# Modulation tiles regrouped: none in steps 16 to 27 of the input projection, ten groups of four ahead of steps 28 to 37, with the weight split of those steps moved

## The chip, the cores and the metric

One core of one Trainium2 chip. The metric is the device time in microseconds (us) of one execution of the kernel; lower is better.

## The reference, cut to what matters

One layer of a diffusion backbone, on 128 context and 256 latent tokens (T = 384 columns, three blocks of 128 rows) of width 2048:

```python
mod = silu(cond) @ w_mod + b_mod                 # 2048 -> 6*2048, for two conditioning vectors
sh_m, sc_m, g_m, sh_f, sc_f, g_f = split(mod, 6)
h = rmsnorm(x, g0) * (1 + sc_m) + sh_m
u = h @ w_in                                     # 2048 -> 5120
m = concat(diff_attention, rg_lru, neighbourhood_attention, gqa)(u)
x = x + g_m * rmsnorm(m @ w_out, g1)
h = rmsnorm(x, g2) * (1 + sc_f) + sh_f
a, g = split(h @ w_ffn_in, 2)
x = x + g_f * rmsnorm((silu(g) * a) @ w_ffn_out, g3)
```

All is f32. The large matmuls split each operand into a high part that the fast f32 format holds exactly and the remainder, and add three products: high times high, low times high, high times low.

## The kernel before, in words

**Weight tiles.** All weights come as 284 tiles of 1 MB (128 partitions, 4 x 512 values each), in the order of a list, PLAN (lines 94 to 110). SyncE issues one DMA for each (line 441), in that order, into a ring of six buffers, raw. Ahead of each it waits until the tile that had the buffer is used up (lines 427 to 433). So a transfer that must wait holds back all behind it. The buffer of a tile is the one freed longest ago (tile_slots, line 122), which in this stretch is that of six tiles earlier.

**The steps.** Input and output projection are 56 steps of one GEMM tile each (STEPS). Steps 0 to 15 do the first four column blocks with k outermost; from 16 on a column block takes four steps. Steps 40 to 55 are the output projection. A step from 4 on (step_tile, line 914) is 36 matmuls of 512 columns: for each of three row blocks tb, four k and three products (lines 934 to 936). Behind each row block comes a "gap" with whatever attention work stands in a hand-made table, GAPS (line 149): gap g = 3s + tb. Before its first matmul the step waits for both halves of the split tile.

**The split.** hi (line 452) is ScalarE's: two copies of 128x1024 from raw to whi, a ring of two tiles. lo (line 1218) is VectorE's: two subtractions raw - whi, written over the raw buffer as wlo. In the loops over s (lines 666 and 1541) both engines run, in this order: the third gap of step s-1; the eviction of modulation rows (ScalarE, rows_out, if a group ends in this step) or the convolution of the recurrence (VectorE); hi or lo of tile s+1; the other work of the step; gap(s, 0), and on VectorE mod_out; gap(s, 1). Each engine takes its instructions in this order.

**Modulation.** mod is made in 22 groups; group m from 4 on has four tiles of 1 MB, each used by four matmuls of 32 weight columns x 512 (mod_tile, line 798; each is two instructions in the profile), side by side in four parts of the array. mod_tiles (line 84) says which tiles stand ahead of step s: four in steps 2 and 3, two in each of steps 4 to 35. When a group is complete, ScalarE copies it (rows_out, line 463), TensorE turns it with four transposes (mod_turn, line 811) behind the first row block of that step, and VectorE reduces it to modc (mod_out, line 1273). From group 10 on all groups use PSUM bank 3, and the first tile waits until the group before is in modc (line 802). Groups 12 to 21 are not needed before step 39.

**Recurrence and attention.** Steps 16 to 27 also carry the RG-LRU recurrence: four rounds of three steps. TensorE turns its input ahead of the first step of round 0 and behind steps 18, 21 and 24 (lru_turn, line 979: six transposes; the first waits until VectorE has added the partial sums of step 15, part_add, line 1359). The gates' matmuls (lru_gates, line 991) come behind steps 16, 19, 22 and 25. VectorE runs lru_conv (1373), lru_decay (1385) and lru_scan (1404) in the three steps of a round, each behind or ahead of the lo of its step; ScalarE its tanh, exp and sqrt; GpSimd gelu, norms and rope. Attention starts at gap 85 (step 28). Once head group D is done (gap 108, in step 36) GpSimd issues the load of kvC and sixteen small loads of the bias table.

Of the kernel before, what the change touches and what calls it, by code (L numbers as in the profile page):

```python
# [32 lines left out]
KG = 4  # L33
# [16 lines left out]
KH = KD // 2  # L50
KG2 = FK // KG
EARLY = 4
IN_STEPS = IN_N * KG
OUT_N = D // NC
OUT_KG = [1, 3, 0, 2]
STEPS = IN_STEPS + OUT_N * KG

FINE = 4
MOD_K0 = [16, 0, 18, 2] + [4 * j for j in [5, 1, 6, 2, 7, 3] + list(range(8, 20))]
# [10 lines left out]
def in_step(s):  # L70

    return (s % EARLY, s // EARLY) if s < EARLY * KG else (s // KG, s % KG)


def step_key(s):

    if s < IN_STEPS:
        return ("in",) + in_step(s)
    if s < STEPS:
        return ("out", s % OUT_N, OUT_KG[(s - IN_STEPS) // OUT_N])  # L80
    return ("up", 0, 0)


def mod_tiles(s):

    if s < 2:
        return 0, []
    if s < EARLY:
        return FINE + s - 2, [0, 1, 2, 3]
    m, first = 4 + s // 2, s % 2 * 2  # L90
    return (m, [first, first + 1]) if m < len(MOD_K0) else (0, [])


def tile_plan():
# [54 lines left out]
def attention_gaps():  # L149
# [23 lines left out]
    for h in range(4):  # L173
        conv[TB * IN_STEPS + h] = ("D", h)
        conv[TB * IN_STEPS + 18 + h] = ("A", h)
    return {g: [task[1:] for task in sorted(tasks)] for g, tasks in gaps.items()}, conv
# [9 lines left out]
CONV_NO = {_key: _i for _i, (_g, _key) in enumerate(sorted(CONV.items()))}  # L186
A_SCALE = {TB * IN_STEPS + 14 + _h: _h for _h in range(4)}
K_SLOT = [0, 0, 1, 1] + [hd % 2 for hd in range(4, 12)]
# [9 lines left out]
def build(nc, wst, xt_d, x_p, x_s, cdiff, cna, cgqa, c, c_ctx, lam_w, gate_w, na_rpb, qk_g, par_d, tables_d,  # L198
# [101 lines left out]
    with ExitStack() as ctx:  # L300
# [94 lines left out]
        def in_bank(s, tb):  # L395

            return (4 if s < EARLY * KG and s % 2 else 0) + tb

# [4 lines left out]
        def last_step(n):  # L403

            return EARLY * (KG - 1) + n if n < EARLY else KG * n + KG - 1

        GATES_AT = {("in",) + in_step(EARLY * KG + 3 * i): i for i in range(4)}

        ENDS = {}
        for st in range(STEPS):  # L410
            if st < EARLY * KG or st >= IN_STEPS or st % KG == KG - 1:
                ENDS[st] = len(ENDS)
# [38 lines left out]
        def _(act):  # L451
# [26 lines left out]
            def part_out(n):  # L478

                for tb in range(TB):  # L480
                    if tb < TB - 1:
                        act.wait_ge(acc_ps, 2 * n + tb + 1)
                    else:
                        act.wait_ge(w_used, used(*step_key(n // 2 * 2 + 1)) - 1 + n % 2)
                    nc.scalar.activation(U[:, n, tb, :], ps[4 * (n % 2) + tb][:, :], ACT.Copy).then_inc(part_a, 1)
# [180 lines left out]
            for s in range(STEPS):  # L666
                i, phase = (s - EARLY * KG) // 3, (s - EARLY * KG) % 3
                lru = 0 <= i < 4
                m, kgs = mod_tiles(s)
                if s > EARLY * KG:  # L670
                    gap(s - 1, 2)
                if s == 0:
                    rows_out(2)
                    rows_out(3)
                    hi(*step_key(1), bs=(0,))
                    h_shift(2)
                    h_shift(3)
                    hi(*step_key(1), bs=(1,))
                if s == 1:
                    part_out(0)  # L680
                    part_out(1)
                if KG - 1 in kgs:
                    rows_out(m)
                if s == 3:
                    for k in range(KG, 2 * KG):
                        h_shift(k)
                if lru and phase == 0:
                    lru_in(i)
                if s:
                    hi(*step_key(s + 1))  # L690
                if s == EARLY * KG:
                    act.wait_ge(l_setup, 2)
                if s == 3:
                    part_out(2)
                    part_out(3)
                if s in (7, 11):
                    for k in range(s + 1, s + 1 + KG):
                        h_shift(k)
                if lru and phase == 1:
                    lru_gates(i)  # L700
                if lru and phase == 2:
                    lru_sqrt(i)
                if s == EARLY * KG:
                    act.wait_ge(lam_p, 1)
                    nc.scalar.activation(lamt[:, 2:4], lamt[:, 0:2], ACT.Exp).then_inc(lam_e, 1)
                    act.wait_ge(part_d, TB * EARLY * (KG - 1))
                    norm_squares(2, DK, 12, 0)
                if s == EARLY * KG + 2:
                    norm_squares(4, DQ, 0, 6)
                if s in (IN_STEPS - 2, IN_STEPS - 1):  # L710
                    act.wait_ge(w_used, used("in", IN_N - 1, 1))
                    for n in range(2 * (s % 2), 2 * (s % 2) + 2):
                        nc.scalar.activation(h_hi[:, 4 + n, :].rearrange("p (t f) -> p t f", f=P),
                                             u3(BX + n * P, P), ACT.Copy).then_inc(mb_hi, 1)
                if s >= EARLY * KG:
                    gap(s, 0)
                    gap(s, 1)
# [489 lines left out]
        def _(dve):  # L1207
# [10 lines left out]
            def lo(*key, bs=(0, 1)):  # L1218

                t = TILE[key]  # L1220
                g = GEMM_NO[t]
                for b in bs:
                    dve.wait_ge(w_hi, 2 * g + b + 1)
                    V.tensor_tensor(wlo[:, 2 * SLOT[t] + b], raw_of(t)[:, HK * b:HK * b + HK].rearrange("p k n -> p (k n)"),  # L1224
                                    whi[:, 2 * (g % RING) + b].bitcast(F32), ALU.subtract).then_inc(w_lo, 1)
# [315 lines left out]
            for s in range(STEPS):  # L1541
                i, phase = (s - EARLY * KG) // 3, (s - EARLY * KG) % 3
                lru = 0 <= i < 4
                m, kgs = mod_tiles(s)
                n = s - (STEPS - OUT_N)
                if s > EARLY * KG:
                    gap(s - 1, 2)
                if n >= 0:
                    diagonal(G_M, n, 0, 2 * n + 1)
                if s in (2, 3):  # L1550
                    mod_out(m)
                    if s == 2:
                        dve.wait_ge(xr_ok, 1)
                        col_scaled(KG, KG, m).then_inc(xs_ok, 1)
                    else:
                        for k in range(KG, 2 * KG):
                            first_h(k)
                if lru and phase == 0:
                    lru_conv(i)
                if s:  # L1560
                    lo(*step_key(s + 1))
                if n > 0:
                    for tb in range(TB):
                        y1_gate(n - 1, tb)
                if KG - 1 in kgs and EARLY <= s < EARLY * KG:
                    mod_out(m)
                    if m < 10 and m % 2 == 0:
                        dve.wait_ge(xr_ok, m // 2 - 1)
                        col_scaled(KG * (m // 2 - 1), KG, m).then_inc(xs_ok, 1)
                if s == 2:  # L1570
                    softplus()
                if s in (7, 11):
                    for k in range(s + 1, s + 1 + KG):
                        first_h(k)
                if EARLY <= s < EARLY * KG:
                    part_add(s)
                if s >= EARLY * KG:
                    gap(s, 0)
                    if KG - 1 in kgs:
                        mod_out(m)  # L1580
                if lru and phase == 1:
                    lru_decay(i)
                if lru and phase == 2:
                    lru_scan(i)
                if s in (IN_STEPS - 2, IN_STEPS - 1):
                    for b in range(2 * (s % 2), 2 * (s % 2) + 2):
                        dve.wait_ge(mb_hi, b + 1)
                        V.tensor_tensor(h_lo[:, 4 + b, :].rearrange("p (t f) -> p t f", f=P), u3(BX + b * P, P),
                                        h_hi[:, 4 + b, :].rearrange("p (t f) -> p t f", f=P).bitcast(F32),
                                        ALU.subtract).then_inc(mb_lo, 1)  # L1590
                if s == IN_STEPS + 7:
                    dve.wait_ge(mod_col, len(MOD_K0))
                    gain(G_M, 1, False)
                    gain(SC_F, 2, True)
                if s >= EARLY * KG:
                    gap(s, 1)
                if -1 <= n < OUT_N - 1:
                    diagonal(G_M, n + 1, 1, 2 * n + 2)
# [379 lines left out]
```

## Time and profile before

| what | value |
|---|---|
| median of 3 runs | 1799.8 us (1799.41 to 1800.14) |
| the profiled execution, its own time | 1798.27 us |
| its span, first to last instruction | 1796.4 us |
| TensorE (PE) busy, share of the span | 1763.2 us, 98% |
| VectorE (DVE) busy | 947.0 us, 53% |
| ScalarE (ACT) busy | 659.8 us, 37% |
| mean granted TensorE clock | 0.999 |

PE rows are matmuls, PEld rows weight loads, POOL is GpSimd. Matmuls are pipelined: a row's duration is longer than the distance to the next one, so a run of matmuls is read by start to start. In rows of the timeline the brackets at the end give the engine's idle time before the row and what ended it.

### The profile page before, as it was taken

The page shows a single profiled execution, that of the slowest core. Times are in us where ns is not written, and L with a number is a line of the kernel's source. Part 1 is how long each engine was busy: PE and PEld are TensorE (multiplying, and loading weights), DVE is VectorE, ACT ScalarE, POOL GpSimd, SP SyncE. Part 2 cuts the span into 40 slices and gives each one's busy share as a digit, 9 for nine tenths or more (in the row PEclk, how much of TensorE's full clock was granted, in tenths as well). Part 3 has the DMA queues.
Part 4 walks back from the last instruction along what each step waited for, and adds up shares of the span by engine and source line. Part 5 has one row for each costly group of instructions (what it writes and reads, how often), then busy time and mean ns, then how long its engine had stood idle before and what let it go on. Part 6 is the DMA issues. An engine that isn't in the chain of part 4 may idle for free.

```text
span 1796.4 us, 22651 instructions
## 1 busy us (share of the span) xinstructions
PE 1763.2 (98%) x9499; PEld 1526.4 (85%) x9499; DVE 947.0 (53%) x1276; ACT 659.8 (37%) x952; POOL 125.9 (7%) x172
## 2 busy tenths in 40 slices
PE   5999999999999999999999999999999999999998
PEld 4667666677778879999999999999999988888886
DVE  5554578633657677356656633333333455555554
ACT  3422354443464344222222222222222344454542
POOL 1001045420300010000000000000000000000000
PEclk9999999999999999999999999999999999999999
DMA  9988777775322242345454443433333333333331
GB/s 395 349 331 318 299 270 273 294 265 228 114 104 94 104 177 117 118 172 203 167 207 188 182 147 117 140 118 124 135 117 140 119 124 134 117 138 121 121 113 71
DMA packets 47046, 317.37 MB, mean 177 GB/s; under 512 B 5433, under 2 KB 7665, under 8 KB 10017
## 3 DMA queue, kind: packets, MB, share of 16 engines
q1 hardware_dynamic: 44592, 305.35, 45.4%
q0 software_dynamic: 2288, 10.56, 1.8%
q8 instruction: 75, 1.23, 0.3%
q14 instruction: 27, 0.21, 0.0%
q10 hardware_dynamic: 64, 0.02, 0.0%
HBM read 310.52 MB, written 5.39 MB: 176 GB/s over the span
## 4 chain that ended last, share of the span: by engine, by line
PE 93%; DVE 3%; DMA 2%; ACT 1%; issue 0%; POOL 0%; SPq 0%; DVEq 0%; POOLq 0%; ACTq 0%
PE ps L1158 41%; PE ps L934 7%; PE ps L936 7%; PE ps L935 7%; PE ps L828 7%; PE ps L829 7%; PE ps L827 7%; PE ps L806 3%; DMA raw<-in_weights 2%; PE ps L1048 1%; PE ps L1071 1%; DVE wlo L1224 1%; PE ps L1106 1%; PE ps L894 1%; PE ps L896 1%; PE ps L895 1%
## 5 line engine op out<-in xcount | busy, mean ns | idle before, releaser
L1224 DVE TENSOR_TENSOR wlo<-raw,whi 128x1024 fp32r<-128x1024 f32 x376 | 459.8, 1236 | 692.6 <-ACT whi L460 692.1
L460 ACT ACTIVATE whi<-raw 128x1024 fp32r<-128x1024 f32 x376 | 392.3, 1058 | 829.7 <-PE ps L1158 507.0
L1158 PE MATMUL ps<-h_hi,whi 128*128 128x384 f32 x1408 | 471.4, 335 | 0.5 <-DVE h_lo L1303 0.5
L1158 PE MATMUL ps<-h_hi,wlo 128*128 128x384 f32 x1408 | 470.4, 334 | 0.0
L1158 PE MATMUL ps<-h_lo,whi 128*128 128x384 f32 x1408 | 470.3, 334 | 0.0
L1158 PEld LDWEIGHTS ps<-h_hi,whi 128*128 128x128 f32 x1408 | 264.3, 188 | 0.7 <-issue 0.7
L1158 PEld LDWEIGHTS ps<-h_lo,whi 128*128 128x128 f32 x1408 | 264.3, 188 | 0.0
L1158 PEld LDWEIGHTS ps<-h_hi,wlo 128*128 128x128 f32 x1408 | 264.3, 188 | 0.0
L934 PE MATMUL ps<-whi,h_hi 128*128 128x512 f32 x624 | 259.8, 416 | 0.2 <-DVE wlo L1224 0.2
L936 PE MATMUL ps<-wlo,h_hi 128*128 128x512 f32 x624 | 244.5, 392 | 0.0
L935 PE MATMUL ps<-whi,h_lo 128*128 128x512 f32 x624 | 243.6, 390 | 0.0
L827 PE MATMUL ps<-whi,j_hi 128*128 128x512 f32 x516 | 204.0, 395 | 0.0
L829 PE MATMUL ps<-wlo,j_hi 128*128 128x512 f32 x516 | 200.9, 389 | 0.0
L828 PE MATMUL ps<-whi,j_lo 128*128 128x512 f32 x516 | 200.9, 389 | 0.0
L934 PEld LDWEIGHTS ps<-whi,h_hi 128*128 128x128 f32 x624 | 117.2, 188 | 54.6 <-issue 28.7
L936 PEld LDWEIGHTS ps<-wlo,h_hi 128*128 128x128 f32 x624 | 117.1, 188 | 25.9
L935 PEld LDWEIGHTS ps<-whi,h_lo 128*128 128x128 f32 x624 | 117.5, 188 | 25.1 <-issue 1.9
L828 PEld LDWEIGHTS ps<-whi,j_lo 128*128 128x128 f32 x516 | 96.9, 188 | 21.9 <-issue 1.9
L827 PEld LDWEIGHTS ps<-whi,j_hi 128*128 128x128 f32 x516 | 96.9, 188 | 21.8 <-issue 1.9
L829 PEld LDWEIGHTS ps<-wlo,j_hi 128*128 128x128 f32 x516 | 96.9, 188 | 20.1
L1635 DVE TENSOR_TENSOR j_lo<-h3T,j_hi 128x1536 fp32r<-128x1536 f32 x44 | 77.4, 1758 | 8.4 <-ACT j_hi L762 8.4
L1855 POOL TENSOR_TENSOR smalls<-smalls 128x3 f32<-128x3 f32 x2 | 0.4, 188 | 1027.0 <-ACT ps L725 998.2
(257 smaller groups left out, 1363.6 us busy)
## 6 DMA issues: line engine op xcount, KB each, us to landing
raw<-in_weights SPq DMA_DIRECT2D x278, 1024.0 KB, 4.9
raw_x<-in_weights SPq DMA_DIRECT2D x6, 1024.0 KB, 18.5
xT<-in_x_t SPq DMA_DIRECT2D x4, 768.0 KB, 7.0
out<-x_sb SPq DMA_DIRECT2D x6, 512.0 KB, 2.7
x_sb<-in_x_sample POOLq DMA_DIRECT2D x1, 2048.0 KB, 11.0
sbc<-silu_rows POOLq DMA_DIRECT2D x1, 2048.0 KB, 8.2
gw<-in_lru_gate_w SPq DMA_DIRECT2D x4, 256.0 KB, 3.3
out<-U POOLq DMA_DIRECT2D x4, 256.0 KB, 5.6
```

What stands on the lines that cost most here:

```text
L460: nc.scalar.activation(whi[:, 2 * (g % RING) + b], raw_of(t)[:, HK * b:HK * b + HK].rearrange("p k n -> p (k n)"), ACT.Copy).then_inc(w_hi, 1)
L806: ins = nc.tensor.matmul(ps[mod_bank(m)][32 * kk:32 * kk + 32, :], stat[:, 2 * k:2 * k + 32], raw_of(t)[:, kk, :], start=(kg == 0), stop=( ...
L827: nc.tensor.matmul(acc, xh[:, kk + HK * b, xs], wh[:, cols], start=(k == 0), stop=False)
L828: nc.tensor.matmul(acc, xl[:, kk + HK * b, xs], wh[:, cols], start=False, stop=False)
L829: ins = nc.tensor.matmul(acc, xh[:, kk + HK * b, xs], wl[:, cols], start=False, stop=(k == k_last))
L894: nc.tensor.matmul(acc, h_hi[:, k, xs], wh[:, cols], start=(k == 0), stop=False)
L934: nc.tensor.matmul(acc, h_hi[:, k, xs], wh[:, cols], start=begin, stop=False)
L935: nc.tensor.matmul(acc, h_lo[:, k, xs], wh[:, cols], start=False, stop=False)
L936: ins = nc.tensor.matmul(acc, h_hi[:, k, xs], wl[:, cols], start=False, stop=end)
L1158: return nc.tensor.matmul(ps[bank][:, 0:T], w[:, k % KH * P:(k % KH + 1) * P], xs[:, k, :], start=first, stop=last)
L1224: V.tensor_tensor(wlo[:, 2 * SLOT[t] + b], raw_of(t)[:, HK * b:HK * b + HK].rearrange("p k n -> p (k n)"), whi[:, 2 * (g % RING) + b].bitc ...
L1635: V.tensor_tensor(j_lo[v % 2][:, :, :], h3T[:, KG * q:KG * q + KG, :], j_hi[v % 2][:, :, :].bitcast(F32), ALU.subtract).then_inc(jl, 1)
```

## The change

It changes mod_tiles: steps 4 to 15 keep two tiles each, steps 16 to 27 have none, and steps 28 to 37 have all four tiles of groups 12 to 21. PLAN, the order of the transfers and the buffers follow from it; the number of tiles, matmuls and transposes is the same. And for tiles 29 to 37 hi and lo are no longer issued one step ahead, but in the tile's own step, right behind the third gap of the step before: on ScalarE ahead of rows_out. Tile 38 is split one step ahead again, in step 37, behind tile 37.

```diff
@@ -50,6 +50,8 @@
 EARLY = 4
+FOURS = EARLY * KG + 12
+FOURS_END = FOURS + 9
 IN_STEPS = IN_N * KG
@@ -87,8 +89,9 @@
         return 0, []
     if s < EARLY:
         return FINE + s - 2, [0, 1, 2, 3]
-    m, first = 4 + s // 2, s % 2 * 2
-    return (m, [first, first + 1]) if m < len(MOD_K0) else (0, [])
+    if FOURS <= s <= FOURS_END:
+        return 12 + s - FOURS, [0, 1, 2, 3]
+    return (4 + s // 2, [s % 2 * 2, s % 2 * 2 + 1]) if s < EARLY * KG else (0, [])
@@ -679,6 +682,8 @@  (ScalarE)
                 if s == 1:
                     part_out(0)
                     part_out(1)
+                if FOURS <= s - 1 < FOURS_END:
+                    hi(*step_key(s))
                 if KG - 1 in kgs:
                     rows_out(m)
@@ -686,7 +691,7 @@
                 if lru and phase == 0:
                     lru_in(i)
-                if s:
+                if s and not FOURS <= s < FOURS_END:
                     hi(*step_key(s + 1))
@@ -1557,7 +1562,9 @@  (VectorE)
                 if lru and phase == 0:
                     lru_conv(i)
-                if s:
+                if FOURS <= s - 1 < FOURS_END:
+                    lo(*step_key(s))
+                if s and not FOURS <= s < FOURS_END:
                     lo(*step_key(s + 1))
```

## Rows read from the trace of the kernel before

**Rows 1.** The page: span and busy time.

```profile
span 1796.4 us, 22651 instructions
PE 1763.2 (98%) x9499; PEld 1526.4 (85%) x9499; DVE 947.0 (53%) x1276; ACT 659.8 (37%) x952; POOL 125.9 (7%) x172
```

**Rows 2.** Waits of PE, 200 to 470 us: us in total, times, longest.

```profile
PE ps L1061 <- DVE pb L1460: 1.8, 1, 1.8
PE ps L806 <- DVE modc L1280: 1.2, 1, 1.2
```

**Rows 3.** Timeline of PE in step 15: start, duration, engine, line.

```profile
192.50 1.93 PE L806 MATMUL ps<-raw,stat 128*32 128x512 f32 x16
194.35 0.50 PE L934 MATMUL ps<-whi,h_hi 128*128 128x512 f32 x1
...
195.84 0.60 PE L815 MATMUL ps<-par,modrow 128*128 128x128 f32 x4
196.20 0.48 PE L934 MATMUL ps<-whi,h_hi 128*128 128x512 f32 x1
```

**Rows 4.** Timeline of PE in step 3, four modulation tiles in a row.

```profile
64.17 1.92 PE L806 MATMUL ps<-raw_x,stat 128*32 128x512 f32 x16
65.91 1.90 PE L806 MATMUL ps<-raw,stat 128*32 128x512 f32 x16
67.74 0.50 PE L894 MATMUL ps<-whi,h_hi 128*128 128x512 f32 x1
```

**Rows 5.** Timeline of PE, steps 16 and 17, start of steps 28 and 29.

```profile
203.22 1.92 PE L806 MATMUL ps<-raw,stat 128*32 128x512 f32 x16
205.08 0.87 PE L988 MATMUL ps<-par,U 128*128 128x128 f32 x6
205.71 0.47 PE L934 MATMUL ps<-whi,h_hi 128*128 128x512 f32 x1
...
214.00 2.77 PE L998 MATMUL ps<-lru_xc,gw 128*128 128x388 f32 x8
216.70 1.93 PE L806 MATMUL ps<-raw,stat 128*32 128x512 f32 x16
...
343.34 1.93 PE L806 MATMUL ps<-raw,stat 128*32 128x512 f32 x16
...
354.40 1.93 PE L806 MATMUL ps<-raw,stat 128*32 128x512 f32 x16
```

**Rows 6.** Timeline of DVE: step 15's sums, lo of tiles 21, 22, 23.

```profile
202.49 1.88 DVE L1371 TENSOR_TENSOR U<-U,ps 128x512 f32<-128x512 f32 x3
...
255.05 2.36 DVE L1224 TENSOR_TENSOR wlo<-raw,whi 128x1024 fp32r<-128x1024 f32 x2 [6.62 <-ACT whi L460]
...
270.77 3.44 DVE L1224 TENSOR_TENSOR wlo<-raw,whi 128x1024 fp32r<-128x1024 f32 x2
...
282.88 2.35 DVE L1224 TENSOR_TENSOR wlo<-raw,whi 128x1024 fp32r<-128x1024 f32 x2
```

**Rows 7.** Timeline of ACT and then DVE in step 30: hi and lo.

```profile
371.48 2.01 ACT L460 ACTIVATE whi<-raw 128x1024 fp32r<-128x1024 f32 x2 [4.94 <-DMA raw<-in_weights]
...
372.58 2.36 DVE L1224 TENSOR_TENSOR wlo<-raw,whi 128x1024 fp32r<-128x1024 f32 x2 [7.32 <-ACT whi L460]
```

**Rows 8.** Timeline of PE: the tiles ahead of steps 30 and 33.

```profile
366.16 1.92 PE L806 MATMUL ps<-raw,stat 128*32 128x512 f32 x16
...
406.83 1.92 PE L806 MATMUL ps<-raw,stat 128*32 128x512 f32 x16
```

**Rows 9.** Timeline of ACT: last work of gaps 89, 98, 107.

```profile
366.27 0.28 ACT L592 ACTIVATE pT<-ps 128x128 f32<-128x128 f32 x1 [1.21 <-PE ps L1061]
...
408.20 0.19 ACT L603 ACTIVATION_READ_ACCUMULATOR pb<-ps,smalls 128x1 f32 x1
...
448.10 2.00 ACT L460 ACTIVATE whi<-raw 128x1024 fp32r<-128x1024 f32 x2
```

**Rows 10.** Windows: us, PE, PEld, DVE, ACT, POOL busy, PEclk, DMA share, GB/s.

```profile
10.00:20.00 10.00, 5.23 (x88) 4.01 (x92) 6.87 (x7) 3.47 (x5) 0.00 (x0) 1.00 1.02 427
```

**Rows 11.** DMA queue of GpSimd, 445 to 465 us: packets, MB, share.

```profile
q0 software_dynamic: 656, 1.57, 34.0%
```

## The prediction

> **What bounds the kernel now.** I read the page first: TensorE is busy for 98% of the span [rows 1]. Then the waits of PE: from step 16 to step 37 it waits for other engines for little more than 3 us, the two entries shown and one of 0.4 us [rows 2]. So the kernel is bound by TensorE, and what the change can gain is TensorE time itself; what it can lose is any wait that it opens, in full, since nothing later has slack to take it back. Then the timelines of PE, ACT and DVE, step by step, to see what each step costs TensorE and how far ahead of it the split runs.
>
> **The change part by part.** All terms are against the profiled execution (its own time 1798.3 us, span 1796.4 us). That is 1.5 us under the median of the runs.
>
> *TensorE work taken out of steps 16 to 27.* From 203.22 to 343.34 us it takes 140.1 us [rows 5]. A bare step is 205.71 to 214.00, 8.3 us; twelve make 99.5. The four input turns at 0.63 (205.08 to 205.71) make 2.5, the four gate groups at 2.70 (214.00 to 216.70) make 10.8 [rows 5]. What is left, 27.3 us, is what the modulation takes there: 24 tiles, six turns of a group, and the 1.2 us wait of a first tile for modc [rows 2]. It all goes: **-27.3**.
>
> *The same work in steps 28 to 37.* Two tiles take 1.85 us start to start [rows 3], four in a row 3.57 (64.17 to 67.74) [rows 4]. Eight steps go from two to four, 8 x 1.72 = 13.8; steps 36 and 37 get four, 7.1; six more groups turn there, each 0.36 and a slower first matmul, about 0.44 [rows 3], 2.6. **+23.5**. The net of both is -3.8: fewer runs of these tiles, each with its way in and out, and the lost wait. That is the whole gain.
>
> *The first input turn loses its cover.* Now two tiles run from 203.22 to 205.08 while VectorE adds the sums of step 15, which end at 202.49 + 1.88 = 204.37 [rows 5, 6]. Without them the turn could start at 203.2 and has to wait for 204.4: **+1.2**. Between nothing and 1.9 (the cover's whole length).
>
> *VectorE in the recurrence.* Its work of one round, here the second, runs almost without a break from lo of tile 21 at 255.05 to the end of lo of tile 23 at 285.23: 30.2 us [rows 6], of which about 1.5 is idle or mod_out. Call it 28.7. TensorE's round loses its tiles and shrinks to 3 x 8.3 + 0.6 + 2.7 = 28.2 us. So VectorE, with slack now, becomes about even, and late in the rounds in which GpSimd works beside it. lo of tile 22 comes behind the whole of lru_decay, then scan and convolution stand ahead of lo of tile 23 and of the gates' matmuls. Following both engines' orders by these durations I get 1.3 us lost at step 22, about 1 us at the gates behind it, less than 1 us in the third round, nothing in the first and last. The splits themselves don't wait for transfers there (one tile a step). I take **+2.0**; from 0 (slack at the start of each round suffices) to 6 (2 in each of three rounds).
>
> The row of tile 22 shows two subtractions in 3.44 us where 2.36 is usual [rows 6], beside GpSimd's norm. The Trainium skill, SBUF — State Buffer, section "SBUF: two separate sides", says that a VectorE operation with two SBUF inputs and a GpSimd operation lock each other out for a whole instruction; the trace agrees in kind, at 1.1 us for the pair. If every GpSimd operation of a round cost VectorE its full length, it would be the second rival below.
>
> *The split moved behind the gap.* This is the large term. TensorE leaves the third gap of step s-1 and starts on the four tiles at once; call that T. It is ready for the step at T + 3.57 [rows 4]. From the start of hi to the end of lo it takes 371.48 to 374.94, 3.46 us [rows 7]. So hi would have to start at T + 0.1, but ScalarE has the gap's work first. In step 30 the last copy ends 0.4 us after T (366.27 + 0.28 against 366.16) [rows 8, 9]: 0.2 lost. In step 33 the exponential of the gap ends at 408.39, 1.56 after T = 406.83 [rows 8, 9]: 1.4 lost. Behind gap 107, with two exponentials, hi can start at 448.10 [rows 9], 1.7 after the gap: 1.6 lost. Read in this way for the nine steps 29 to 37, the losses are 0.4, 0.2, 1.0, 1.4, 1.4, 0.4, 0.2, 1.6, 0.7: **+7.5**. From 5 (some of these waits overlap with others) to 9 (lo stretched by GpSimd in two or three steps, 1.1 each).
>
> *Transfers.* Steps 28 to 37 now need five tiles each instead of three. At full load the queues move 427 GB/s [rows 10], 2.5 us for a tile. A tile alone takes 5.3 us from the freed buffer (about 366.1) to hi at 371.48 [rows 7, 8]. In the new order the first tile for the next step is freed when the step before ends, and the fifth, the one to split, lands four tiles later: 5.3 + 10 = 15.3 us after it. A step of this stretch takes 13.4 to 13.8 us now (from 366.16 to 406.83 three steps, 13.6 each) [rows 8], and 15.3 to 16 with two more tiles and its wait; hi is wanted about 1 us later still. That just holds. It does not hold for tile 29: step 28 takes 11.06 [rows 5], then 13.2, so the tile lands 1.5 us late, and the load of kvA falls there too: **+2.0**, from 0 to 4. And it does not for tile 37: when head group D is done in step 36, GpSimd's loads take 34% of the engines' time over 20 us, 6.8 us [rows 11], and some 3 of them fall ahead of tile 37, with 1 of slack: **+2.0**, from 0 to 6.
>
> The Trainium skill, DMA: Bandwidth & Descriptors, section "Anatomy of one DMA", gives about 2.0 us plus bytes over 436 GB/s for one DMA, 4.4 us for a tile. By that estimate the fifth tile would land at 14.0, tile 29 would be in time, and the sum about 1.5 smaller; the 5.3 read here includes SyncE's wait and issue, so I keep it.
>
> *At nothing.* The wait of 1.8 us in step 37 [rows 2] comes from GpSimd's bias addition beside VectorE; that falls into the same step again. rows_out behind hi is ready before the first row block ends. The attention's own work has more time per step than before; rope and kvA keep tens of us. SyncE's queue keeps its count; what is queued behind each waiting transfer is in the sum above. hi of tile 38 follows in step 37 behind rows_out and delays gap 111 by 1 to 2 us, behind a row block of 2.7 us.
>
> *Sum:* -27.3 + 23.5 + 1.2 + 2.0 + 7.5 + 2.0 + 2.0 = +10.9. On the profiled execution 1809.2, on the median 1810.7. I say **1810 us**, slower by 0.6%. A measurement of this kernel can tell about 0.2% (3.6 us) from no change.
>
> **The rivals.**
>
> *The cover holds, and it is faster.* If ScalarE is done with the gap when TensorE is, the split hides behind the four tiles in every step; the terms of the split and of tiles 29 and 37 vanish, and with no loss in the recurrence only -3.8 + 1.2 = -2.6 is left: 1797, and 1795 if the 1.8 us wait goes too. It decides at hi starting within 0.1 us of T in all nine steps. For it: six of the nine are within 1 us. Against: 3.46 alone is all of 3.57, and the exponentials wait for maxima of scores that TensorE makes last. Parts of it (losses of 2 or 3 in place of 7.5) give no change. 12% for faster by over 0.2%.
>
> *VectorE bounds the recurrence.* With contention in all rounds and lo always behind decay, 2 to 3 us a round more: 1815. For it: 28.7 against 28.2. Against: rounds one and four have less of it. 12%.
>
> *Transfers bound steps 28 to 37.* If a tile takes 2.8 or 3 us in place of 2.5 among GpSimd's loads and stores, the fifth lands 1 to 2 us later, in seven steps where it just holds: +8 to +12, 1820. 8%.
>
> *Little of it shows.* The terms at their lower ends: -3.8 + 1.2 + 5 + 0 = +2, 1801 to 1803, within 0.2%. 18%.
>
> My forecast's own case has the rest, 50%.
>
> **The numbers.** Slower by over 0.2% takes the forecast, both slow rivals: 70%. Within 0.2% 18%, faster 12%. The range for 8 in 10 reaches from 1799 (lower ends of the costs) to 1818.
>
> **What would show it.** On the changed kernel's waits of PE: step matmuls (L934's line) waiting for lo's wlo nine times, 0.2 to 4 us each, about 11 us in total in steps 29 to 37, longest at 29 or 37; a wait of the input turn for U of about 1.2 us; one or two waits in step 22 or at the gates. The L806 busy time would be a little lower, and steps 16 to 27 would take some 116 us in place of 140. ACT rows of hi in steps 30 to 36 should wait for nothing or for gap work, not for DMA. It is wrong if step matmuls wait for wlo under 3 us in all, or if they wait for raw through hi in most steps (transfers), or if steps 16 to 27 take over 120 us (VectorE).

## The result and the profile after

The changed kernel takes 1812.95 us (median of 4 runs, 1811.8 to 1813.6), the kernel before in the same comparison 1799.97 us; the ratio is 1.0072, with a 95% interval of 1.0054 to 1.0089. So it is slower by 13 us, 0.7%. The profiled execution took 1812.96 us, 14.7 us more than that of before (1798.27).

The page of the changed kernel, span and busy time, against [rows 1]:

```profile
span 1811.2 us, 22651 instructions
PE 1764.4 (97%) x9499; PEld 1530.6 (85%) x9499; DVE 948.8 (52%) x1276; ACT 660.2 (36%) x952; POOL 126.9 (7%) x172
```

No engine does more work: PE is busy 1.2 us longer and the span is 14.8 us longer. The rest is waiting. PE's waits of the changed kernel over the whole execution, in us: total, times, longest (L939 are the step matmuls, L934 before; L993 is the input turn; L1066 turns probabilities, L1061 before):

```profile
PE ps L939 <- DVE wlo L1229: 14.0, 11, 5.4
PE ps L1066 <- DVE pb L1465: 2.5, 1, 2.5
...
PE ps L993 <- DVE U L1376: 0.9, 1, 0.9
```

The waits for wlo were 0.2 us before. The 1.2 us wait for modc in [rows 2] is gone. Where they are, in the timeline of PE of the changed kernel; the bracket is the wait, and L811 are the modulation tiles (L806 before):

```profile
205.10 0.84 PE L993 MATMUL ps<-par,U 128*128 128x128 f32 x6 [0.87 <-DVE U L1376]
...
262.79 0.47 PE L939 MATMUL ps<-whi,h_hi 128*128 128x512 f32 x1 [1.26 <-DVE wlo L1229]
...
318.34 3.64 PE L811 MATMUL ps<-raw,stat 128*32 128x512 f32 x32
...
331.60 3.64 PE L811 MATMUL ps<-raw,stat 128*32 128x512 f32 x32
340.61 0.77 PE L939 MATMUL ps<-whi,h_hi 128*128 128x512 f32 x1 [5.37 <-DVE wlo L1229]
...
355.97 0.47 PE L939 MATMUL ps<-whi,h_hi 128*128 128x512 f32 x1 [0.18 <-DVE wlo L1229]
...
372.13 0.47 PE L939 MATMUL ps<-whi,h_hi 128*128 128x512 f32 x1 [0.88 <-DVE wlo L1229]
...
405.83 0.47 PE L939 MATMUL ps<-whi,h_hi 128*128 128x512 f32 x1 [1.36 <-DVE wlo L1229]
...
453.31 0.47 PE L939 MATMUL ps<-whi,h_hi 128*128 128x512 f32 x1 [1.62 <-DVE wlo L1229]
```

Step 28 starts at 318.34 and not at 343.34 [rows 5], so the emptied steps give 25.0 us. Then each of steps 29 to 37 waits for its own split: 5.37, 0.18, 0.88, 1.36, 1.36, 0.40, 0.18, 1.62 and 0.68 us, 12.0 in all; without step 29 it is 6.7.

Step 29 holds the surprise. Windows of the changed kernel around its wait (us; PE, PEld, DVE, ACT, POOL busy; granted clock; DMA share; GB/s):

```profile
334.00:338.00 4.00, 1.24 (x12) 0.13 (x4) 0.90 (x1) 1.99 (x3) 3.73 (x6) 0.93 0.99 399
338.00:340.60 2.60, 0.00 (x0) 0.02 (x1) 2.50 (x2) 1.78 (x3) 2.52 (x2) 0.50 1.01 425
340.60:345.00 4.40, 4.39 (x12) 3.49 (x13) 0.00 (x0) 0.00 (x0) 4.09 (x6) 0.59 1.01 423
```

The transfers run at full rate, 399 to 425 GB/s. During the wait the granted clock falls to 0.50, that is 1.2 GHz, and stays there into the step, until about 344.2 us. From its first matmul (340.61) to the tiles ahead of step 30 (352.15) the step takes 11.5 us, where it took 9.9 before (354.40 + 1.85 to 366.16) [rows 3, 5, 8].

Two timelines of the changed kernel, ACT and then DVE, show why tile 29 is so late:

```profile
336.01 2.00 ACT L463 ACTIVATE whi<-raw 128x1024 fp32r<-128x1024 f32 x2 [3.82 <-DMA raw<-in_weights]
```

```profile
337.10 3.40 DVE L1229 TENSOR_TENSOR wlo<-raw,whi 128x1024 fp32r<-128x1024 f32 x2 [10.88 <-ACT whi L463]
```

hi waits for the transfer until 336.0, 4.4 us after the tiles of its step began; and lo, beside GpSimd's rope, takes 3.4 us in place of 2.36.

The second fall comes in step 37 (GpSimd's bias addition runs from 476.96 to 481.53). DVE first, then PE:

```profile
477.38 4.17 DVE L1285 TENSOR_TENSOR modc<-modc,par 128x8 f32<-128x8 f32 x1
```

```profile
482.86 0.55 PE L1066 MATMUL ps<-par,pb 128*128 128x128 f32 x3 [2.52 <-DVE pb L1465]
...
485.28 0.63 PE L940 MATMUL ps<-whi,h_lo 128*128 128x512 f32 x1
485.71 0.63 PE L941 MATMUL ps<-wlo,h_hi 128*128 128x512 f32 x1
...
488.20 0.38 PE L1076 MATMUL ps<-kvA,pT 128*128 128x128 f32 x2
```

A window of this stretch:

```profile
485.00:487.00 2.00, 2.00 (x7) 1.52 (x6) 0.44 (x1) 2.00 (x6) 0.00 (x0) 0.50 0.19 78
```

An operation that takes 0.2 us alone on VectorE lasts 4.2 us here. TensorE waits 2.5 us (1.8 before), and then, at a granted clock of 0.50, its matmuls are 0.43 us apart where 0.23 is usual; that row block costs another 1.6 us.

### The profile page after: what moved, and what is told of

Same layout as the page of the kernel before. It is cut to its first block, busy times and chain, and to the rows that moved or that the text cites. A ratio compares the mean times of both kernels' runs of the same rounds, so it can differ in the third digit from the quotient of the medians.

```text
span 1811.2 us, 22651 instructions
## 1 busy us (share of the span) xinstructions
PE 1764.4 (97%) x9499; PEld 1530.6 (85%) x9499; DVE 948.8 (52%) x1276; ACT 660.2 (36%) x952; POOL 126.9 (7%) x172
## 4 chain that ended last, share of the span: by engine, by line
PE 90%; DVE 4%; DMA 3%; ACT 1%; issue 1%; POOL 0%; SPq 0%; DVEq 0%; ACTq 0%; POOLq 0%
PE ps L1163 40%; PE ps L939 7%; PE ps L941 7%; PE ps L940 7%; PE ps L834 6%; PE ps L833 6%; PE ps L832 6%; DMA raw<-in_weights 3%; DVE wlo L1229 2%; PE ps L811 2%; PE ps L1053 1%; PE ps L1076 1%; ACT whi L463 1%; PE ps L1111 1%; PE ps L899 1%
## 5 line engine op out<-in xcount | busy, mean ns | idle before, releaser
L939 PE MATMUL ps<-whi,h_hi 128*128 128x512 f32 x624 | 260.5, 417 | 14.0 <-DVE wlo L1229 14.0
L939 PEld LDWEIGHTS ps<-whi,h_hi 128*128 128x128 f32 x624 | 118.1, 189 | 62.8 <-DVE wlo L1229 24.4
```

Of the source, the lines that this page charges most:

```text
L939: nc.tensor.matmul(acc, h_hi[:, k, xs], wh[:, cols], start=begin, stop=False)
```

## The experiments

All ratios below are against the kernel before, run on the same chip in the same comparison (1799.2 to 1799.4 us).

**1. The split one step ahead again.**

```diff
-                if FOURS <= s - 1 < FOURS_END:
-                    hi(*step_key(s))
-                if s and not FOURS <= s < FOURS_END:
+                if s:
                     hi(*step_key(s + 1))
```

and the same for lo.

> The changed kernel with hi and lo again one step ahead in every step; the groups of four stay. Theory A (the late split costs what TensorE waits for wlo, but with five tiles a step it could not be earlier, since the tile lands some 15 us after the step before ended): ScalarE would now stand at hi before the gap's work of the same step, the attention's copies and exponentials come 5 to 10 us late in each of nine steps, and the time is 1850 to 1900 us. Rival B (the place of the split is itself the loss): 1803 to 1807 us, without the nine waits for wlo. Between 1808 and 1830 neither holds as stated.

Measured: 1884.1 us, ratio 1.0471 (1.0451 to 1.0490). ACT's waits from 319 to 484 us:

```profile
ACT whi L463 <- DMA raw<-in_weights: 75.0, 7, 13.2
```

Theory A holds. With five tiles a step, ScalarE at hi waits up to 13 us for a transfer, and the gap's copies and exponentials stand behind it: TensorE now waits 6 to 7 us in most steps for pT, kT, qT, pb or U. The queues are not full while this goes on: the share of DMA time is 0.45 to 0.74 in each 20 us from 340 to 480 us. Read from the orders of the engines, TensorE frees the buffers late, since it waits for the gap's work, and ScalarE holds that work back until the transfer is there. The granted clock is 0.83 to 0.87 in the same stretch, so part of the 71 us over the changed kernel is the clock. With five tiles a step the late split is the cheaper of the two places.

**2. The split ahead of the third gap.**

```diff
                 m, kgs = mod_tiles(s)
+                if FOURS <= s - 1 < FOURS_END:
+                    hi(*step_key(s))
                 if s > EARLY * KG:
                     gap(s - 1, 2)
...
-                if FOURS <= s - 1 < FOURS_END:
-                    hi(*step_key(s))
```

and the same for lo.

> The changed kernel with hi and lo of tiles 29 to 37 ahead of the third gap of the step before, not behind it, on both engines. Theory A (in steps 30 to 37 the split is late because ScalarE has the gap's copies and exponentials first; the tile itself has landed): the eight waits of step matmuls for wlo in steps 30 to 37, 6.7 us in all, shrink to under 1.5 us in all, that of step 29 stays at about 5 us; 1807 to 1808 us. Rival C (in those steps the tile lands only just in time, so the order does not matter): waits as before and 1812 to 1814 us, or more where the gap's work is now held up.

Measured: 1809.1 us, ratio 1.0059 (1.0046 to 1.0071). The waits that are left, in the timeline of PE of this kernel, all those from step 29 on:

```profile
341.01 0.77 PE L939 MATMUL ps<-whi,h_hi 128*128 128x512 f32 x1 [5.42 <-DVE wlo L1229]
...
372.92 0.47 PE L939 MATMUL ps<-whi,h_hi 128*128 128x512 f32 x1 [0.65 <-DVE wlo L1229]
...
433.98 0.47 PE L939 MATMUL ps<-whi,h_hi 128*128 128x512 f32 x1 [0.34 <-DVE wlo L1229]
...
449.86 0.47 PE L939 MATMUL ps<-whi,h_hi 128*128 128x512 f32 x1 [0.40 <-DVE wlo L1229]
...
467.42 0.47 PE L939 MATMUL ps<-whi,h_hi 128*128 128x512 f32 x1 [2.20 <-DVE wlo L1229]
482.06 0.55 PE L1066 MATMUL ps<-par,pb 128*128 128x128 f32 x3 [3.66 <-DVE pb L1465]
```

In steps 30 to 36 the waits fall from 6.0 to 1.4 us: there it was the gap's work ahead of hi, as theory A has it. But step 37 now waits 2.2 us in place of 0.7. ACT in that step:

```profile
463.87 2.00 ACT L463 ACTIVATE whi<-raw 128x1024 fp32r<-128x1024 f32 x2 [3.02 <-DMA raw<-in_weights]
```

The tile lands 2.3 us after the step's tiles began (461.57): the load that GpSimd issues in step 36, which I had forecast, shows once the gap's work no longer hides it. The expected time was missed by 1 us. The median is 4 us under that of the changed kernel, by the ratios 2 us, and their intervals overlap, so the gain in time is not settled. The traced execution (1812.24 us) gained only 0.7: it waits 3.0 us less for wlo, but 1.1 more for pb in step 37, and the slow clock costs 0.8 more in step 29 (12.4 us from its first matmul to the next tiles). What this run shows is whose waits they were.

**3. The first group ahead of step 27.**

```diff
-    if FOURS <= s <= FOURS_END:
-        return 12 + s - FOURS, [0, 1, 2, 3]
+    if s == FOURS - 1 or FOURS < s <= FOURS_END:
+        return 12 + max(s - FOURS, 0), [0, 1, 2, 3]
```

> The changed kernel with group 12 ahead of step 27 and none ahead of step 28; groups 13 to 21 stay ahead of steps 29 to 37. Theory A (tile 29 comes late because five tiles and the load of kvA are queued behind the end of step 27 and step 28 is only 13.3 us long; the wait of 5.4 us lets the clock fall): with the queue spread, the wait in step 29 falls from 5.4 to under 1.5 us, the granted clock stays at full in step 29, and the time falls by 5 to 6.5 us, to 1806.5 to 1808. Rival D (the lateness is handed on: the first step with five tiles behind it waits, whichever it is): a wait of 3 to 5 us appears in step 30 or at the tiles ahead of it, and the time stays at 1811 to 1813. The eight waits of steps 30 to 37 stay at 6.7 us in either.

Measured: 1809.2 us, ratio 1.0053 (1.0040 to 1.0065); the profiled execution 1807.95. PE:

```profile
336.03 0.47 PE L939 MATMUL ps<-whi,h_hi 128*128 128x512 f32 x1 [1.29 <-DVE wlo L1229]
...
350.66 0.47 PE L939 MATMUL ps<-whi,h_hi 128*128 128x512 f32 x1 [1.14 <-DVE wlo L1229]
```

The wait in step 29 falls from 5.4 to 1.3 us and the clock stays full there (1.00 from 330 to 353 us). Step 30 waits 1.1 in place of 0.2 and steps 30 to 37 together 8.2 in place of 6.7 us; so of theory D there is 1.5 us, of theory A the rest. In step 37 of this execution the clock falls too, behind a wait of 2.2 us.

**4. kvA loaded later.** Its line moved behind the two rope calls of group A.

> The changed kernel with the load of kvA issued behind the rope of group A instead of ahead of it. Theory A (kvA's 512 KB stand in the queues between the end of step 27 and tile 29, 1.2 us of full rate): the wait in step 29 falls from 5.4 to about 4 us, and the time by 1 to 2 us, to 1811 to 1812; the clock may still fall behind that wait. Rival E (kvA shares no time with tile 29): no difference.

Measured: 1808.3 us, ratio 1.0053 (1.0037 to 1.0068). The wait in step 29 is 3.71 us, as expected, 1.7 less. The window of this kernel in which step 29 waits and the next one:

```profile
334.00:338.00 4.00, 0.50 (x8) 0.00 (x0) 3.04 (x2) 3.64 (x4) 3.77 (x4) 1.00 1.02 358
338.00:340.60 2.60, 2.39 (x11) 1.99 (x11) 0.11 (x1) 0.00 (x0) 2.52 (x4) 1.00 0.97 400
```

The clock stays full behind 3.7 us, so the step is at 9.9 us again. By the ratios the gain is 3.4 us, where 1 to 2 were expected, but the intervals overlap. The traced execution (1806.21 us) gained 6.8: 3.3 in step 29, wait and clock together, and 2.9 in step 37, which this edit does not touch. There the wait for pb was 1.2 in place of 2.5 us, and the clock stayed full. So not all of the gain is kvA's.

**5. The wait filled.**

```diff
+                if s == FOURS + 1:
+                    keep_busy(7, 20)
                 parts = list(halves(TILE[step_key(s)]))
```

> The changed kernel with twenty small matmuls into a free PSUM bank ahead of step 29's wait for wlo; their result is not used. They take about 4.5 us and the wait is 5.4. Theory A (the wait lets the granted clock fall to 1.2 GHz for the first matmuls of step 29, 1.6 us lost on top of the wait): what is left of the wait is about 0.9 us, the granted clock stays at full through 340 to 352 us, step 29 from its first matmul to the tiles of step 30 takes 9.9 us in place of 11.5, and the time is 1 to 2 us lower, 1811 to 1812. Rival F (the slower step 29 has another cause, such as transfers or GpSimd's rope beside it): step 29 takes 11.5 us again.

Measured: 1810.6 us, ratio 1.0064 (1.0051 to 1.0078). The first step matmul starts 9.04 us behind the tiles in this kernel (331.74 to 340.78) and 9.01 in the changed kernel, so lo is no earlier. PE:

```profile
331.74 3.64 PE L811 MATMUL ps<-raw,stat 128*32 128x512 f32 x32
...
340.78 0.47 PE L941 MATMUL ps<-whi,h_hi 128*128 128x512 f32 x1 [0.74 <-DVE wlo L1231]
350.64 3.64 PE L811 MATMUL ps<-raw,stat 128*32 128x512 f32 x32
```

The clock stays at 1.00, and the step takes 9.86 us in place of 11.54. So the clock is what slowed step 29, at 1.7 us, and rival F falls: transfers and rope are beside it as before. In step 37, where nothing was added, the clock stayed full as well this time, behind a wait of 2.7 us. The medians differ by less than their intervals can tell.

**6. The edits of 2, 3 and 4 together.**

> The changed kernel with the three edits of the second to fourth experiment together: split ahead of the third gap, first group ahead of step 27, kvA later. Theory A: the wait in step 29 goes (5.4, and the clock loss behind it, 1.6), those of steps 30 to 36 go to about 1.4 in all, that of step 37 stays at 2.2 because tile 37 then waits for its transfer among GpSimd's small loads; 1802 to 1805 us, still above the kernel before by 0.1 to 0.3%, since the input turn (0.9) and step 22 (1.3) lose and merging ten pairs of runs brings only 2 to 4 us. Rival: waits of 1 us or more come back in most of steps 30 to 36 as the late tile shows behind the gap's work; 1806 to 1809.

Measured: 1805.6 us, ratio 1.0036 (1.0023 to 1.0050): half the loss is gone, 0.6 us above the top of theory A. PE waits for wlo in four places (1.3 us in step 22, 2.1 in step 30, 2.2 in step 31, 0.2 in step 35), and ACT shows for the two longest that the tile is late:

```profile
348.15 2.00 ACT L463 ACTIVATE whi<-raw 128x1024 fp32r<-128x1024 f32 x2 [3.47 <-DMA raw<-in_weights]
...
365.55 2.00 ACT L463 ACTIVATE whi<-raw 128x1024 fp32r<-128x1024 f32 x2 [4.96 <-DMA raw<-in_weights]
```

The modulation tiles of these steps began at 346.00 and 363.31. Without the other waits the steps are shorter, and in two of them five tiles no longer fit: the transfers are the next bound there, as the rival said for most of the steps. Step 37, where theory A had 2.2 us, does not wait for wlo at all. Waits of 0.9 (input turn), 1.3 (step 22) and 3.1 (step 37's pb, with a fall of the clock behind it) stay.

**7. Merged runs without the rest of the change.** From the kernel before:

```diff
     m, first = 4 + s // 2, s % 2 * 2
+    if s >= EARLY * KG:
+        return (m, [0, 1, 2, 3]) if s % 2 == 0 and m < len(MOD_K0) else (0, [])
```

> The kernel before, with one change: groups 12 to 21 stand as four tiles ahead of every second step (16, 18 to 34) instead of two ahead of each of steps 16 to 35; the split stays one step ahead everywhere. It merges as many runs as the change did, without its costs. Theory A: the merging is worth 2 to 4 us (ten times 0.1 to 0.35, and the wait of 1.2 us for modc), there is no wait for wlo over 0.5 us, and the input turn keeps its cover; 1795 to 1797.5 us. Rival G (VectorE is so near TensorE in the recurrence that every step without tiles brings a wait): waits for wlo of 1 to 3 us in steps 19 to 27 and 1797.5 to 1800 us.

Measured: 1803.7 us, ratio 1.0023 (1.0013 to 1.0033). Neither theory: there is one new wait of more than 0.7 us, at the first merged step. ACT and PE:

```profile
204.48 2.00 ACT L462 ACTIVATE whi<-raw 128x1024 fp32r<-128x1024 f32 x2 [8.34 <-DMA raw<-in_weights]
```

```profile
208.28 4.92 PE L808 MATMUL ps<-raw,stat 128*32 128x512 f32 x32 [3.94 <-DVE modc L1282]
```

Tile 16 is queued behind four new tiles instead of two, hi of tile 16 waits 8 us, and behind it, in VectorE's order, come lo, the reduction of group 11 and so the tiles of group 12. The four tiles take 4.9 us, in place of 3.64: the clock is down here too (0.50 from 208 to 210 us). From step 18 on, the merging pays, but little: from the tiles of step 18 to those of step 34 it is 190.8 us (233.41 to 424.19), where the kernel before takes 192.5 (227.43 to 419.89), and 1.2 of these 1.7 us are the wait for modc of before. Step 18 itself begins 6.0 us late.

**8. The same from step 4 on.**

> As the run before, from step 4 on: all groups 6 to 21 as four tiles ahead of even steps 4 to 34. Theory A (sixteen merged pairs): 1 to 2 us less than the run before, 1793.5 to 1796 us. Rival H (steps 4 to 15 are bound by transfers at 390 GB/s, and the next step's tile now stands behind four): waits for wlo or raw in steps 4 to 9 of 2 us or more, and as slow as the kernel before or slower.

Measured: 1803.9 us, ratio 1.0026 (1.0017 to 1.0035). PE's waits from 60 to 205 us:

```profile
PE ps L934 <- DVE wlo L1224: 4.9, 3, 2.3
```

They were 0.2 before, though 0.8 of the 4.9 is at a place (90 us) where experiments 7, 9 and 10 wait 1.1 to 1.2 us too, with steps 4 to 15 unchanged. The longest, 2.3 us at 105 us, is rival H's, and so is the time; the wait for modc at step 16 is gone. The third, 1.8 us at 191 us, stands ahead of step 15 and not in steps 4 to 9, so the rival holds in part.

**9 and 10. The alternation from step 18, and from step 28.**

> As the alternation from step 16, but starting at step 18: steps 16 and 17 keep two tiles each, groups 13 to 21 stand ahead of even steps 18 to 34. Theory A (that run lost what merging gained at its first merged step, where tile 16 was queued behind four tiles, so that lo, the sums of step 15 and modc came late; the rest was 3 us faster): the wait for modc at step 16 is gone; the same lateness moves to step 18, where the recurrence has less to lose; 1796 to 1799 us. Rival (VectorE's decay of round 0 now starts behind the late lo of tile 18 and step 19 waits for it): 1799.5 to 1803.

Measured: 1802.9 us, ratio 1.0019 (1.0011 to 1.0028), in the rival's range, but not by its mechanism: step 19 does not wait. The first merged step waits 1.5 us for modc, as theory A had it, and three more waits of 0.8 to 0.9 come up in steps 24, 25 and 28, for U and for wlo. The traced execution (1800.99 us) is the shortest of its eleven.

> As the run before, but starting at step 28: the recurrence keeps two tiles ahead of every step, groups 18 to 21 stand ahead of steps 28, 30, 32 and 34. Theory A: four merged pairs, 0.35 us each, and no new wait over 1 us; 1797.5 to 1799.5 us, too little to tell from no change. Rival: the splits that now come behind four queued tiles delay the attention's gap work, 1800 to 1803.

Measured: 1806.1 us, ratio 1.0037 (1.0023 to 1.0051). Both expectations missed. The loss is again at the first merged step; ACT and PE:

```profile
344.77 2.00 ACT L462 ACTIVATE whi<-raw 128x1024 fp32r<-128x1024 f32 x2 [9.00 <-DMA raw<-in_weights]
...
348.57 5.34 PE L808 MATMUL ps<-raw,stat 128*32 128x512 f32 x32 [4.61 <-DVE modc L1282]
```

The order is that of experiment 7: hi of tile 28 waits 9 us for its transfer, and lo and the reduction to modc stand behind it on VectorE. The wait and the slow clock behind it (the tiles take 5.3 in place of 3.64 us) make 6.3 us.

So no version tried here beats the kernel before. In experiment 7 merging gained 1.7 us over eight pairs, and the late first step lost more than three times that.

## Why the prediction was right, point by point

The forecast was +10.9 us on the profiled execution; it was +14.7.

| step of the prediction | forecast | in the trace after |
|---|---|---|
| tiles taken out of steps 16 to 27 | -27.3 | -28.1 |
| tiles put into steps 28 to 37 | +23.5 | +23.9 |
| input turn without cover | +1.2 | +0.9 |
| VectorE in the recurrence | +2.0 | +1.3 |
| split behind the gap | +7.5 | +7.1 |
| tile 29 late | +2.0 | +5.0 |
| tile 37 late | +2.0 | 0 |
| clock falls behind two waits | none | +3.3 |
| longer wait in step 37 | 0 | +0.7 |

The rows add up to +14.1 us; with the 0.9 of the next sentence added and the 0.4 of the last one taken off, that is the 14.6 us by which gap 119 comes later. The first row is 25.0 plus the two waits below it and 0.9 us by which step 15 ends later than before (its last matmul starts at 203.84, not 202.91). That stretch has not been changed, and over the kernels of these experiments its end moved by up to 1.9 us (204.79 in experiment 6), so I count it to no step. The second is 39.6 us, by which the stretch from step 28 to the end of gap 119 grew (343.34 to 493.08 before, 318.34 to 507.67 after), less the waits and the clock, with the 0.4 us wait of before that went.

Part of the nearness is luck. The rows that were too low (tile 29, the clock, the wait in step 37 and the tiles put in) miss 7.4 us in all, and those that were too high (tile 37, the recurrence and the other three) take 4.2 of that back. The falls of the clock come and go from run to run, as told below.

*The split behind the gap* was right in size and place. Its nine losses add up to 7.3 us, not to the 7.5 that went into the sum. For steps 30 to 37 it had 0.2, 1.0, 1.4, 1.4, 0.4, 0.2, 1.6, 0.7; measured were 0.18, 0.88, 1.36, 1.36, 0.40, 0.18, 1.62, 0.68. Reading the end of ScalarE's work in each gap of the old trace and adding 3.46 us gave them. Experiment 2 shows the cause, experiment 1 that going a step ahead is no way out.

*The recurrence*: the wait at step 22 came as forecast (1.3); those at the gates and in the third round did not.

*Tile 29* was mis-sized: with the clock, it is the step of the sum that failed. I had the tile 15.3 us behind the end of step 27 and 2.0 us for everything beyond. It came 17.7 us behind (318.3 to 336.0), lo took 3.4 instead of 2.36 us, and the wait beyond the 0.4 of the gap was 5.0. Experiment 4 gives 1.7 us of it to kvA, experiment 3 shows that a freer queue takes nearly all of it away. From 318.34 to 336.0 us SyncE's queue moved 6.0 MB and GpSimd's 0.5, where five tiles are 5.2 MB; so 0.8 MB of something else, probably of the next tile, went beside them. Tile by tile it was not settled what held the rest.

The rule of the Trainium skill, DMA: Bandwidth & Descriptors, section "Anatomy of one DMA", stands there for DMAs that GpSimd issues, and these tiles are issued by SyncE. By the estimate from it the tile would have come 14.0 us behind, which is further off than 15.3. The trace has 17.7 and does not agree with the estimate, but kvA and SyncE's own waits are in these 17.7 us.

*Tile 37* cost nothing, because the gap before it (1.6 and 0.7 us in steps 36 and 37) hid what lateness there was. Experiment 2 took the gap away and 2.2 us showed; in experiment 6, in which step 36 came 4 us earlier, none did. The term was about right by itself and wrong in a sum: two things that end the same wait do not add.

*The clock* was missing: the sum had no term for what follows a wait, and two falls cost 3.3 us.

The rivals' conditions held nowhere: TensorE waited for wlo in all nine steps, steps 16 to 27 took 115 us (203.2 to 318.3), and hi in steps 30 to 37 did not wait for transfers.

## What to carry to other kernels

When work that covered something moves away, list what it covered: here two tiles covered the sums of step 15, and four tiles of 3.6 us were to cover a split of 3.5 us that starts only when another engine has finished its own part. Such a cover must be compared start to start, with the other engine's last instruction in the trace. And a new order of transfers is felt at its first step, where the queue behind it is longest: in experiments 7, 9 and 10 the merged tiles held up the first merged step by 1.5 to 4.6 us and later ones by at most 0.9.

## What the runs showed that I had not expected

The granted clock fell to 1.2 GHz behind waits of 5.4 us (the changed kernel and experiment 2), 4.6 (experiment 10), 3.9 (7), 3.7 (2), 3.1 (6), 2.5 (the changed kernel), 2.3 (8), 2.2 (3) and 1.6 us (8). It did not fall behind others of 3.7 us (4), 2.7 (5), 2.1 and 2.2 (6), 2.1 (7) and 1.6 us (9). So the length of the wait alone does not decide it. Experiments 8 and 9 have the same wait of 1.6 us at the same place, in step 37; their windows behind it, in this order:

```profile
474.00:476.00 2.00, 2.00 (x6) 1.62 (x5) 0.18 (x2) 1.82 (x6) 0.00 (x0) 0.50 0.41 172
474.00:476.00 2.00, 2.00 (x11) 1.63 (x10) 0.23 (x2) 1.70 (x6) 0.00 (x0) 1.00 0.35 143
```

Each fall cost 1.3 to 2.5 us on top of the wait, mostly 1.5 to 1.7. With twenty small matmuls in the wait of 5.4 us it did not fall, in the one execution traced. The traced executions of the changed kernel and of experiment 5 differ in this way in step 37, by 1.6 us, with the same instructions there. The runs of the merged kernels spread more (1802.2 to 1808.3 in experiment 8) than those of the kernel before beside them (1798.4 to 1802.0); that the clock causes the spread was not tried.

And a VectorE operation on eight columns took 4.17 us beside one long GpSimd operation of 4.57 us, which the Trainium skill, SBUF — State Buffer, section "SBUF: two separate sides", describes as a lock for a whole instruction; here the trace agrees with it: GpSimd's began first (476.96), and VectorE's ended 0.02 us after it (481.55 against 481.53).
